# Two-layer expert network on one core: where slot tables and gathers stand in a unit, and the order of the units

## The reference, cut to what matters

```python
def swiglu(x, wg, wu, wd):
    return (jax.nn.silu(x @ wg) * (x @ wu)) @ wd

def moe(h, w_router, e_bias, w_gate, w_up, w_down, ws_gate, ws_up, ws_down):
    ...
    _, eidx = lax.top_k(choice, TOP_K)
    w = jnp.take_along_axis(scores, eidx, axis=1)
    w = w / jnp.sum(w, axis=-1, keepdims=True) * ROUTED_SCALE
    routed = grouped_experts(xt, eidx, w, w_gate, w_up, w_down)
    shared = swiglu(xt, ws_gate, ws_up, ws_down)
    return (routed + shared).reshape(B, S, D)
```

## Time and profile before

| | |
|---|---|
| median of 3 runs | 2744.18 us (2742.7 to 2750.13) |
| profiled execution, span | 2743.8 us |
| TensorE busy | 2625.9 us, 96% |
| VectorE, ScalarE busy | 56%, 37% |
| HBM read | 962.36 MB |

### The profile page before, as it was taken

How to read it: one execution, slowest core, us unless ns; L and a number is a source line. 1 busy time by engine, 2 the same in 40 slices (tenths; PEclk the granted TensorE clock), 3 DMA queues, 4 the chain that set the end, 5 groups by cost and what they waited for, 6 DMA issues and landing times.

```text
span 2743.8 us, 49811 instructions
## 1 busy us (share of the span) xinstructions
PE 2625.9 (96%) x20578; PEld 2001.9 (73%) x20578; DVE 1536.1 (56%) x2614; ACT 1003.0 (37%) x1373; POOL 273.9 (10%) x317
## 2 busy tenths in 40 slices
PE   8999999999899989999999999999999999999998
PEld 5877556556567776665566588898788888988887
DVE  5875333343326663333332376679666666878665
ACT  4433222222225542222222243456433533573433
POOL 1401222221200011222212000000000000000000
PEclk9999999999999999999999999999999999999999
DMA  9965999999998438999999865455555555445552
GB/s 361 282 243 214 375 378 377 395 376 374 408 398 280 163 123 323 380 397 390 379 383 395 317 197 192 155 166 187 169 186 195 192 186 189 164 148 196 170 190 102
DMA packets 274158, 733.76 MB, mean 267 GB/s; under 512 B 45264, under 2 KB 186744, under 8 KB 215328
## 3 DMA queue, kind: packets, MB, share of 16 engines
q1 hardware_dynamic: 229408, 706.78, 69.5%
q0 software_dynamic: 37056, 17.69, 2.6%
q10 hardware_dynamic: 7488, 6.34, 0.8%
HBM read 962.36 MB, written 1.05 MB: 351 GB/s over the span
## 4 chain that ended last, share of the span: by engine, by line
PE 81%; DVE 4%; DMA 3%; ACT 3%; issue 2%; SPq 0%; DVEq 0%; ACTq 0%
PE G L1782 18%; PE Y L1471 5%; PE Y L1472 5%; PE Y L1473 5%; PE U L1802 5%; PE B L1802 4%; DMA wide<-in_moe_w_gate_dram 3%; PE B L1495 3%; PE U L1495 3%; PE G L1495 3%; PE M L1495 3%; PE U L1471 2%; PE G L1471 2%; PE U L1472 2%; PE U L1473 2%
## 5 line engine op out<-in xcount | busy, mean ns | idle before, releaser
L2274 DVE TENSOR_TENSOR part_lo<-ring,part_hi 128x2048 fp32r<-128x2048 f32 x240 | 547.7, 2286 | 281.7 <-ACT part_hi L1090 281.4
L1090 ACT ACTIVATE part_hi<-ring 128x2048 fp32r<-128x2048 f32 x240 | 459.1, 1914 | 489.6 <-PE Y L1473 250.1
L1782 PE MATMUL G<-wide,gathered 128*32 128x256 f32 (+1 forms) x4288 | 464.6, 382 | 24.0 <-issue 23.8
L1782 PE MATMUL G<-arena,gathered 128*32 128x256 f32 (+1 forms) x3392 | 464.8, 382 | 11.4 <-DMA wide<-in_moe_w_gate_dram 10.0
L1782 PEld LDWEIGHTS G<-wide,gathered 128*32 128x32 f32 (+1 forms) x4288 | 271.9, 115 | 105.1 <-issue 39.1
L1782 PEld LDWEIGHTS G<-arena,gathered 128*32 128x32 f32 (+1 forms) x3392 | 253.8, 116 | 91.7 <-issue 21.3
L1471 PE MATMUL Y<-part_hi,rows_hi 128*128 128x512 f32 x608 | 239.3, 394 | 6.2 <-DVE rows_lo L2286 3.6
L1472 PE MATMUL Y<-part_lo,rows_hi 128*128 128x512 f32 x608 | 237.2, 390 | 0.0
L1473 PE MATMUL Y<-part_hi,rows_lo 128*128 128x512 f32 x608 | 236.9, 390 | 0.0
L1194 ACT ACTIVATE swi<-G 128x256 f32<-128x256 f32 x72 | 27.6, 384 | 532.8 <-PE G L1782 532.8
L2535 DVE SCALAR_TENSOR_TENSOR swi<-G,slot_gate,swi 128x256 f32<-128x256 f32 x72 | 34.8, 484 | 307.3 <-ACT swi L1194 302.5
(11 more groups left out here) (618 smaller groups left out, 5765.7 us busy)
## 6 DMA issues: line engine op xcount, KB each, us to landing
wide<-in_moe_w_down_dram SPq DMA_DIRECT2D x128, 1024.0 KB, 8.6
ring<-in_ffn_w_up_dram SPq DMA_DIRECT2D x88, 1024.0 KB, 5.3
arena<-in_moe_w_gate_dram SPq DMA_DIRECT2D x72, 1024.0 KB, 7.7
wide<-in_moe_w_up_dram SPq DMA_DIRECT2D x72, 1024.0 KB, 9.5
wide<-in_moe_w_gate_dram SPq DMA_DIRECT2D x56, 1024.0 KB, 8.8
arena<-in_moe_w_up_dram SPq DMA_DIRECT2D x56, 1024.0 KB, 11.3
ring<-in_ffn_w_down_dram SPq DMA_DIRECT2D x44, 1024.0 KB, 4.9
ring<-in_w_in_dram SPq DMA_DIRECT2D x40, 1024.0 KB, 5.3
```

Source lines behind the costliest of these rows:

```text
L1090: eng.activation(part_hi[:, n % SPLIT, :], ring[:, slot, :], ACT.Copy).then_inc(hi_ready, 1)
L1782: last = mm(bank["G"][first:first + width, part, :], lhsT=gathered[p // 2 % 2][:, k, at:at + width], rhs=units[tile][:, k, :], start=(k == ...
L2274: eng.tensor_tensor(part_lo[:, n % SPLIT, :], ring[:, slot, :], part_hi[:, n % SPLIT, :].bitcast(F32), ALU.subtract).then_inc(lo_ready, 1)
```

## The change

The table of slots of every unit but the first is transposed into bank G, right after `turn_hidden(p)`, and not into M after `down(p)`; VectorE reads it right after `turned_hidden_out(p)`. All four scatters of unit p-1 stand behind `up(p)`; both gathers move behind the slot tables, just ahead of `down(p)`, with U ahead of M (for unit 0 the gather into U stays ahead of `turn_hidden`). ScalarE drains U ahead of M. `up` waits for both drains. The last two units, which have no gathers, put their fourth scatter there. The units' order becomes: MM MM, then twice (MLO LLOO MLO T MLO LLOO MLO T LLOO MLO LLOO T MLO LLOO MLO LLOO T). There are still 36 units and 8 T; the others are 2 MM, 14 MLO and 12 LLOO, where there were 18 MLO and 10 LLOO. The new T units are 5, 9, 13, 18, 22, 26, 30 and 35; before, they were 0, 1, 7, 13, 19, 25, 31 and 35.

```diff
-    kinds = ["T"] * 2
-    for _ in range(5):
-        kinds += ["MLO", "LLOO", "MLO", "MLO", "LLOO", "T"]
-    kinds += ["MLO"] * 3 + ["T"]
+    kinds = ["MM", "MM"]
+    for _ in range(2):
+        kinds += ["MLO", "LLOO", "MLO", "T", "MLO", "LLOO", "MLO", "T", "LLOO", "MLO", "LLOO", "T"]
+        kinds += ["MLO", "LLOO", "MLO", "LLOO", "T"]
...
+def slot_bank(p):
+    return "G" if p else "M"
...
-        seq += late + fills + [f"T{p}"] + ([f"S{p + 1}"] if p + 1 < NP else [])
+        seq += late + [f"T{p}"] + fills
...
                     if nb < BATCHES:
+                        gather_out(nb, f + 1, "U")
                         gather_out(nb, f)
-                        gather_out(nb, f + 1, "U")
...
                 def slot_tables(p):
+                    bk = slot_bank(p)
                     eng.wait_ge(gated_ready, NP * m + p + 1)
-                    wait_free(eng, "M", f"{key}S{p}")
+                    wait_free(eng, bk, f"{key}S{p}")
...
-                    late = True
+                    more = nb < BATCHES
                     if m == 0 and p in COLUMN_PAIRS:
                         late_columns(COLUMN_PAIRS[p])
                     elif p in ROW_PAIRS:
                         gain_row_half(ROW_PAIRS.index(p))
+                    if p == 0:
+                        gather(nb, f + 1, "U")
                     else:
-                        late = False
-                    if nb < BATCHES:
-                        for more, bk in ((1, "U"), (0, "M")) if late else ((0, "M"), (1, "U")):
-                            gather(nb, f + more, bk)
-                    if p:
-                        scatter(p - 1, 0, 0)
-                        scatter(p - 1, 0, 1)
-                        scatter(p - 1, 1, 0)
+                        for t, half in HALVES if more else HALVES[:3]:
+                            scatter(p - 1, t, half)
                     turn_hidden(p)
-                    if p:
-                        scatter(p - 1, 1, 1)
-                    down(p)
                     if p + 1 < NP:
                         slot_tables(p + 1)
+                    if not more:
+                        scatter(p - 1, *HALVES[3])
+                    elif p:
+                        gather(nb, f + 1, "U")
+                    if more:
+                        gather(nb, f)
+                    down(p)
...
                     if p == 0:
                         choose(1)
-                    tables_out(p)
+                        tables_out(0)
...
                     turned_hidden_out(p)
+                    if p + 1 < NP:
+                        tables_out(p + 1)
```

More of the change, by code:

```diff
@@ L252, in book_all @@
             b.own("M", event)
-        b.book("G", key + "pairs", NP)
         for p in range(NP):
+            b.book("G", f"{key}pair{p}")
+            if p + 1 < NP:
+                b.own("G", f"{key}S{p + 1}")
             if p // 2 + 1 < BATCHES:
@@ L1762, in slot_tables @@
                 def slot_tables(p):
+                    bk = slot_bank(p)
                     eng.wait_ge(gated_ready, NP * m + p + 1)
-                    wait_free(eng, "M", f"{key}S{p}")
+                    wait_free(eng, bk, f"{key}S{p}")
                     for t in range(TT):
-                        last = eng.transpose(Mf[:, 0, t * P:(t + 1) * P], gated_select[p % 2][:, t, :], ident[:])
-                    last.then_inc(filled["M"], 1)
+                        last = eng.transpose(bank[bk][:, 0, t * P:(t + 1) * P], gated_select[p % 2][:, t, :], ident[:])
+                    last.then_inc(filled[bk], 1)
                 def up(p, steps):
                     if steps[0] == 0:
-                        if p:
-                            wait_drained(eng, "U" if p > 1 else "M", f"{key}g{p // 2}_3")
-                        wait_free(eng, "G", pairs, p)
+                        if p == 1:
+                            wait_drained(eng, "M", f"{key}g0_3")
+                        elif p:
+                            wait_drained(eng, "U", f"{key}g{p // 2}_3")
+                            wait_drained(eng, "M", f"{key}g{p // 2}_2")
+                        wait_free(eng, "G", f"{key}pair{p}")
                     for step in steps:
@@ L1787, in turn_hidden @@
                 def turn_hidden(p):
-                    wait_drained(eng, "G", pairs, p)
+                    wait_drained(eng, "G", f"{key}pair{p}")
                     wait_free(eng, "M", f"{key}T{p}")
@@ L1882, in experts @@
                         gain_row_half(ROW_PAIRS.index(p))
-                    else:
-                        late = False
-                    if nb < BATCHES:
-                        for more, bk in ((1, "U"), (0, "M")) if late else ((0, "M"), (1, "U")):
-                            gather(nb, f + more, bk)
-                    if p:
-                        scatter(p - 1, 0, 0)
-                        scatter(p - 1, 0, 1)
-                        scatter(p - 1, 1, 0)
+                    if p == 0:
+                        gather(nb, f + 1, "U")
+                    else:
+                        for t, half in HALVES if more else HALVES[:3]:
+                            scatter(p - 1, t, half)
                     turn_hidden(p)
-                    if p:
-                        scatter(p - 1, 1, 1)
-                    down(p)
                     if p + 1 < NP:
                         slot_tables(p + 1)
+                    if not more:
+                        scatter(p - 1, *HALVES[3])
+                    elif p:
+                        gather(nb, f + 1, "U")
+                    if more:
+                        gather(nb, f)
+                    down(p)
                 for t, half in ((0, 0), (1, 0), (0, 1), (1, 1)):
@@ L2445, in experts @@
             def experts(m):
-                key, pairs = f"moe{m}", f"moe{m}pairs"
+                key = f"moe{m}"
                 odd = b.at["down", key] % 2
@@ L2504, in tables_out @@
                 def tables_out(p):
[L2505 to L2508, removed]
+                    bk = slot_bank(p)
+                    table = bank[bk][:, 0, :]
+                    wait_full(eng, bk, f"{key}S{p}")
+                    eng.tensor_reduce(slot_gate[:, p % 2:p % 2 + 1], table, AX.X, ALU.max)
+                    eng.tensor_scalar(turned_select[:, (2 - 2 * odd + p) % 4, :], table, 0.0, None, ALU.is_gt)\
+                       .then_inc(drained[bk], 1)
                 def picks():
@@ L2533, in gated_hidden @@
                     eng.wait_ge(silu_ready, NP * m + p + 1)
-                    wait_drained(eng, "M", f"{key}S{p}")
+                    wait_drained(eng, slot_bank(p), f"{key}S{p}")
                     eng.scalar_tensor_tensor(out=swi[:, 2 + p % 2, :], in0=bank["G"][:, 1, :], scalar=slot_gate[:, p % 2:p % 2 + 1],
```

## The result

The changed kernel takes 2753.39 us (median of 7 runs, 2750.66 to 2768.33) against 2744.18 us: 1.0049 times the kernel before, 95% interval 1.0035 to 1.0064. It is slower by 9 us, clear of noise; forecast were 2734 us and a range of 2712 to 2750. The profiled execution has a span of 2751.7 us, 7.9 us more than before.

The account below looks back on a forecast made before the run. Both TensorE and DMA were taken as nearly full in the expert stretches. Inside of units -2, starts with unit 0 +1.4, order -6 in layer 1 and -3 in layer 0 gave -9.6 us: 2734 us, range 2712 to 2750.

Parts of the forecast that it names:

- order of units: Between units of both layers: T spread among shorter heavy runs cut load stalls, -6 us in layer 1, -3 in layer 0.
- the starts: Start of each layer: up(0) needs four loads where two did, +1.5 us a layer (0 to 4), +3.0 for both.
- unit 0: Unit 0 of each layer: gathering into U earlier removes the 0.92 us wait, -0.8 us a layer (0 to -0.9).
- What a T gives back: At a T between heavy units: three loads instead of six let loads catch up by 2 to 3 us.
- What the load rate is: Expert loads: 414 GB/s, 2.53 us per MiB, so a heavy unit's six take 15.2 us against a 15.3 us step.
- The inside of a unit: Each unit: copy wait -0.21, slot table -0.12, new stall of down for U +0.32; about -0.03, -2 us in 68 units.
- its sign of being wrong: Profile after: wrong if steps grow by more than 0.2 us in layer 1, or layer 0 alone moves over 10 us.
- The rule that a change of tiling mode drains TensorE: Heavy units: two fewer mode changes would save some -0.1 us each, -10 us over both layers instead of -2.
- Layer 0: Layer 0's stalls: two more useful T against uncovered real O blocks, -3 us (-8 to +7); silu 0 to 35 near 569 us.
- loads decide anyway: Rival, both layers: TensorE's time hardly counts where loads are behind; only layer 1 gains, -3 us, 2741 us; chance 0.26.
- The larger wait: Rival, at down on bank U: a longer wait every unit, decisive from 0.47 us, 2758 to 2776 us; chance 0.12.

Follow-up runs that it names:

- order alone: Kernel before with only the new order of units, the inside of a unit as before: 2749.86 us, ratio 1.0023.
- inside alone: Changed kernel with the old order of units, so only the inside of a unit differs from the kernel before: 2747.71 us, ratio 1.0017.
- both, again: The changed kernel run again with no edit: 2757.86 us, ratio 1.0051 to the kernel before.
- both, a T first: Changed kernel with units 0 and 5 exchanged in the order, so a T comes first and an MM stands at unit 5: 2750.91 us, ratio 1.0021.
- early gather, old order: Changed kernel with the old order; gather into U right behind up, fourth scatter behind the slot tables, before the gather into M: 2741.04 us, ratio 0.9990.
- early gather, new order: Changed kernel, new order kept, with the gather into U right behind up and the fourth scatter behind the slot tables: 2749.17 us, ratio 1.0020.
- early gather, a T first: Changed kernel with the gather into U right behind up, fourth scatter behind the slot tables, and the order beginning T, MM: 2747.07 us, ratio 1.0009.
- all T at the head: Kernel before with seven T at the head, then 28 heavy units, then the last T: 2762.92 us, ratio 1.0066.

## Why the prediction was wrong

**The step that failed is the term "order of units", with the start that belongs to it.** The prediction had +3.0 us for the starts, -1.6 for unit 0 and -9 for the stalls, -6 of them in layer 1. The marks of each profile, both layers together, and the mean granted clock of all executions of each version show what came:

| kernel | ratio | first load to silu 1, us | silu 1 to silu 35, us | clock |
|---|---|---|---|---|
| before | 1 | 68.42 | 1081.93 | 0.9908, 0.9904 |
| order alone | 1.0023 | 73.03 | 1077.88 | 0.9897 |
| inside alone | 1.0017 | 64.34 | 1084.32 | 0.9908 |
| both (the changed kernel) | 1.0049 | 72.72 | 1082.04 | 0.9891 |
| both, again | 1.0051 | 74.15 | 1088.66 | 0.9892 |
| both, a T first | 1.0021 | 65.40 | 1089.54 | 0.9911 |
| early gather, old order | 0.9990 | 64.34 | 1077.07 | 0.9917 |
| early gather, new order | 1.0020 | 77.30 | 1086.30 | 0.9892 |
| early gather, a T first | 1.0009 | 65.41 | 1089.26 | 0.9905 |
| all T at the head | 1.0066 | 63.50 | 1106.52 | 0.9905 |

(The clocks before are those of the executions beside the first and the second group of runs.) With the old inside of a unit, the new order costs 4.6 us at the starts and gives back 4.05 of the 9 behind them. With the new inside, which makes the start with a T 4.1 us shorter, it costs 8.4 and 9.8 us at the starts, and behind them it gives 2.3 in one profile and takes 4.3 in the other; with the early gather it costs 13.0 and 9.2. The clock goes with it: the orders that begin with MM have 0.9891 to 0.9897, those that begin with a T 0.9904 to 0.9917, and the exchange of units 0 and 5 alone moves it from 0.9891 and 0.9892 to 0.9911, and with the early gather from 0.9892 to 0.9905. The two groups differ by some 0.0014, which times the span is about 4 us, an estimate of what the clock costs if TensorE were the bound throughout.

*What a T gives back* was put at 2 to 3 us and fitted to the stalls of the kernel before. From silu 1 to silu 35 of layer 1 it takes 533.98 us with all T at the head, 527.58 before and 525.73 with the order alone: the five T between heavy units are worth 6.4 us, 1.3 each, and two more 1.9 us, 0.9 each. (Four of the T also take a late load.) These are single profiles. Part of what loads could use at a T is lost. In the kernel before, DMA has a share of 0.84 in the step from unit 7, a T, to unit 8 of layer 1 and 1.00 in the next (columns as in the earlier trace rows); in the first of them SP waits 7.3 us until a place has been read (columns as in the earlier trace rows), so 2.4 us of DMA's time go unused:

```profile
1131.30:1146.34 15.04, 14.99 (x165) 9.18 (x164) 6.55 (x16) 3.55 (x7) 0.00 (x0) 1.00 0.84 318
1146.34:1161.64 15.30, 15.25 (x189) 8.79 (x190) 5.78 (x22) 3.56 (x7) 2.97 (x3) 1.00 1.00 391
```
```profile
SPq L918 <- PE B L1802: 7.3, 1, 7.3
```

The steps of layer 1 from one silu to the next, taken apart by kind (each sum is the layer less its first and last step and its steps at a T), show where T act:

| kernel | steps heavy to heavy | their sum, us | mean, us | undisturbed, us |
|---|---|---|---|---|
| before | 22 | 347.2 | 15.78 | 15.31 |
| order alone | 19 | 300.0 | 15.79 | 15.30 |
| inside alone | 22 | 348.4 | 15.84 | 15.19 |
| both (the changed kernel) | 19 | 300.8 | 15.83 | 15.18 |
| both, again | 19 | 301.4 | 15.86 | 15.21 |
| both, a T first | 21 | 331.6 | 15.79 | 15.18 |
| early gather, old order | 22 | 346.3 | 15.74 | 15.06 |
| early gather, new order | 19 | 308.4 | 16.23 | 15.06 |
| early gather, a T first | 21 | 334.9 | 15.95 | 15.06 |
| all T at the head | 27 | 430.1 | 15.93 | 15.31 |

In nine of the ten profiles a step from heavy to heavy takes 15.7 to 15.95 us, whatever the order and the inside of a unit; the tenth has 16.23, of which one fall of the clock explains 1.7 of some 8 us and the rest is open. More T do not make these steps shorter: the order alone has the 15.79 of the kernel before. They make them fewer, 19 for 22, and a step at a T has no stall. The fit had one equation (runs of five lose 2 us) for two unknowns, the lag and the credit, and I chose the pair that suited three-unit runs losing nothing. In the changed kernel each run of layer 1 between two T loses 0.5 to 3 us again, runs of three 0.5 to 1.1 where the prediction had nothing.

*What the load rate is* was read from 20 us in which a late load and real O blocks kept the queues fullest, 414 GB/s; over a long run it is 390. At that rate a heavy unit is bound by loads (15.9 us) and not by TensorE (15.3), which the text had as nearly even. What TensorE saves in a heavy unit then hardly counts, and what it pays in a step at a T counts in full: from the kernel before to the early gather in the old order the table's last column fell by 0.25 us, its mean by 0.04.

*The start*: mechanism and place were right (two gates and two ups at `up(0)`), the size was half. 0.8 us were put for the gates; the wait is 2.45 us in layer 0 and 2.86 in layer 1. The landing of 5.3 us was that of the dense layers' loads, and the first two expert loads of layer 0 leave 1.15 us apart in the profile after. And the wait can have a second price that the text didn't have, the clock: it fell to its lower level behind the wait ahead of the first `up` in four of the eight starts with MM first that were profiled, 1.4 us of the start in the first of them. Before, it fell behind silu 0 in both layers, so that against the kernel before this price is not extra in the first profile. That the order of loads makes the start late was shown by the exchange of units 0 and 5.

**The inside of a unit** had the right mechanism and nearly the right size: the new stall is 0.40 us (0.32 forecast), of which the slower release, 0.14 us where 0.06 was taken, is the difference; heavy to heavy fell by 0.13 us, T to heavy rose by 0.14, and heavy to T rose from 15.14 to 15.38, which is more than the 0.2 us that the prediction named as its sign of being wrong. The mean over a layer's undisturbed steps changed by nearly nothing, as forecast (-0.03; the prediction's own terms, -0.21 - 0.12 + 0.32, make -0.01, or -0.7 us and not -2). What it missed is that the steps do not weigh alike: the gain lies in heavy units, which wait for loads anyway, and the loss beside T, where nothing hides it: 14 steps x 0.19 = 2.7 us a layer. The run with the inside alone, 4.7 us slower (0.6 to 8.8), agrees in sign only: its profile has 4.1 us less at the starts and 2.4 us more behind them, so the cause of the 4.7 is argued here and not shown. In layer 1 of that run the 22 heavy steps grew by 1.2 us in sum, though the undisturbed ones among them are 0.12 us shorter. The unit 0 term (-0.8 us a layer) depends on the order: from silu 0 to silu 1, layer 1, it was -2.0 us with the old one (17.76 to 15.80) and -0.5 with the new one (17.25 to 16.77). It is also not the wait for U alone: before, the clock fell in this step in both layers (0.72 over 6 us in layer 0, so some 1.7 us lost, an estimate), and with the inside alone it stayed at 1.00.

*The rule that a change of tiling mode drains TensorE* (the Trainium skill, "TensorEngine Tiling (Array Packing)", Key Properties) would have given another -8 us. Undisturbed steps agree with it in direction, in heavy units that lost two changes of mode (-0.13 us net of the 0.19 us larger wait). In heavy to T, where the slot table no longer stands between the modes, the step grew by 0.24. The time shows nothing of the gain; that those units wait for loads (15.8 us a step) is the likely reason. No run tried the modes by themselves.

*Layer 0* had -3 us and one profile shows -2.7, the other +3.2, so that the first comes near the forecast of 569 us is luck. Its real O blocks cost somewhat more than before: silu 29 to silu 35 takes 102.6 and 104.4 us in the two profiles (104.2 with the order alone) against 101.7, with the same kinds of steps.

*The rivals*: "loads decide anyway" was the nearest, with the right mechanism, but it was given a gain of 3 us because it let the start's cost only eat the gain and not outweigh it. "The larger wait" needed 0.47 us a unit to end slower; 0.40 was measured, and slower it came out all the same, since the 9.6 us it was set against weren't there.

## What to carry to other kernels

Where two resources are nearly even, measure which one a long undisturbed run is bound by (here 15.93 us a step against 15.31) before spending a saving on the other. What a light unit gives back to loads that run ahead is counted from two arrangements, not fitted to one. And what a stage needs before its first instruction is waited for at every start: put the unit with the fewest loads there, and look at what its old place loses by it.

## What was not expected of the hardware

The 2.45 us wait ahead of the first `up` cost more than itself: in 244 to 250 us the granted clock was 0.72 and matmuls took 0.63 us, where 0.38 is usual. The kernel before waited 0.58 us there, and its clock fell only later, behind the wait of 2.10 us. With the order alone the wait was 2.74 us in the same place and the matmul behind it took 0.40 us (timeline of PE):

```profile
240.07 0.40 PE L1782 MATMUL G<-arena,gathered 128*64 128x256 f32 x1 [2.74 <-DMA wide<-in_moe_w_gate_dram]
```

In the eight starts with MM first the clock fell behind waits of 2.42, 2.45, 2.68 and 2.83 us and stayed up behind 1.99, 2.74, 2.86 and 3.00, so the drop does not follow from the wait's length alone.

And loads that skip their rows aren't free: in the run of heavy units above, POOL's queue moved 0.06 MB in 15,207 packets, which took 2.1% of the DMA engines' time. DMA was at 0.99 with 390 GB/s there, where the stretch with real O blocks had moved 414 at 1.00; that the skipped rows take the difference was not tried.
